# Gate products beside the latent attention: eight half passes in place of four whole ones

## The reference, cut to what matters

```python
h = rms_norm(x, g_mix)
z = h @ w_in
c_q, c_kv, k_rope, u2, q_nsa, kv_nsa, gate_nsa, gate_mix = jnp.split(z, SPLIT_IDX, axis=-1)
o_a = mla_mixer(c_q, c_kv, k_rope, ...)          # latent attention, 8 heads, causal, 512 x 512 scores
...
g_a, g_b, g_c = jnp.split(jax.nn.sigmoid(gate_mix.astype(jnp.float32)).astype(dt), N_MIXERS, axis=-1)
x = x + (g_a * o_a + g_b * o_b + g_c * o_c) @ w_out
```

## Time and profile before

| what | value |
|---|---|
| median of 3 runs | 3433.9 us (3432.43 to 3441.73) |
| the profiled execution, its own time | 3434.53 us |
| its span in the profile | 3432.7 us |
| PE busy, share of the span | 3374.2 us, 98% |
| PE weight loads busy | 2778.3 us, 81% |
| DVE, ACT, POOL busy | 59%, 42%, 46% |
| mean granted TensorE clock | 0.992 of full |
| chain that ended last, by engine | PE 83%, DVE 8%, ACT 5%, issue 2% |
| latent attention, layer 0 and layer 1 | from about 234 us and from about 1163 us on, some 50 us each |

### The profile page before, as it was taken

One profiled execution on the slowest core, in us unless ns is written; L12 is line 12 of the kernel. 1 busy time (PEld: TensorE's weight loads), 2 busy tenths in 40 slices (PEclk: granted clock), 3 DMA queues, 4 the chain that ended last, 5 costly groups with the idle time before them and its releaser, 6 DMA issues.

```text
span 3432.7 us, 44131 instructions
## 1 busy us (share of the span) xinstructions
PE 3374.2 (98%) x15776; PEld 2778.3 (81%) x15776; DVE 2018.2 (59%) x3204; ACT 1437.5 (42%) x2515; POOL 1587.8 (46%) x829
## 2 busy tenths in 40 slices
PE   9999999999999999999999999999999999999998
PEld 7877887888888778878888887888888877888887
DVE  6775666112367756751223676768964676768953
ACT  3256743332333567442323447333333447333332
POOL 3447454444434574644443641435544641435543
PEclk9999999999999999999999999999999999999999
DMA  4311123222332111322343221532344221432322
GB/s 173 110 56 44 38 93 111 98 98 94 107 114 99 50 44 50 115 94 96 109 145 124 69 87 56 179 128 98 134 138 146 68 87 50 173 134 104 134 94 103
DMA packets 96890, 346.65 MB, mean 101 GB/s; under 512 B 12640, under 2 KB 13408, under 8 KB 96096
## 3 DMA queue, kind: packets, MB, share of 16 engines
q1 hardware_dynamic: 96736, 344.62, 29.1%
HBM read 338.15 MB, written 6.29 MB: 100 GB/s over the span
## 4 chain that ended last, share of the span: by engine, by line
PE 83%; DVE 8%; ACT 5%; issue 2%; SPq 1%; POOL 0%; DMA 0%; ACTq 0%; DVEq 0%; POOLq 0%
PE ps L392 41%; PE ps L817 15%; PE ps L1425 4%; PE ps L550 4%; ACT arena L1298 3%; PE ps L403 3%; DVE split L1269 2%; PE ps L1705 2%; PE ps L1205 1%; PE ps L789 1%; PE ps L1915 1%; DVE ps L1261 1%; PE ps L805 1%; PE ps L1228 1%; PE ps L461 1%
## 5 line engine op out<-in xcount | busy, mean ns | idle before, releaser
L315 POOL TENSOR_TENSOR weights_lo<-arena,weights_hi 128x1024 fp32r<-128x1024 f32 x462 | 1176.8, 2548 | 1450.6 <-ACT weights_hi L285 1349.7
L285 ACT ACTIVATE weights_hi<-arena 128x1024 fp32r<-128x1024 f32 x490 | 516.8, 1055 | 614.4 <-PE ps L817 354.9
L392 PE MATMUL ps<-moving_hi,weights_hi 128*128 128x512 f32 x2144 | 536.5, 392 | 3.3 <-ACTq L278 1.8
L392 PE MATMUL ps<-moving_lo,weights_hi 128*128 128x512 f32 x2144 | 531.0, 390 | 0.0
L392 PE MATMUL ps<-moving_hi,weights_lo 128*128 128x512 f32 x2144 | 529.9, 389 | 0.0
L392 PEld LDWEIGHTS ps<-moving_hi,weights_hi 128*128 128x128 f32 x2144 | 399.7, 188 | 89.6 <-ACT weights_hi L285 4.0
L392 PEld LDWEIGHTS ps<-moving_hi,weights_lo 128*128 128x128 f32 x2144 | 402.2, 188 | 82.8
L392 PEld LDWEIGHTS ps<-moving_lo,weights_hi 128*128 128x128 f32 x2144 | 401.3, 188 | 83.9 <-issue 1.0
L336 DVE TENSOR_TENSOR moving_lo<-arena,moving_hi 128x512 fp32r<-128x512 f32 x196 | 202.7, 1084 | 223.3 <-ACT moving_hi L331 223.2
L534 POOL TENSOR_TENSOR weights_lo<-arena,weights_hi 128x512 fp32r<-128x512 f32 x80 | 105.1, 1326 | 270.8 <-ACT weights_hi L285 185.7
L2719 DVE SCALAR_TENSOR_TENSOR arena<-ps,arena 128x512 f32 x64 | 44.1, 691 | 294.2 <-PE ps L392 272.6
(11 more groups left out here) (396 smaller groups left out, 5426.9 us busy)
## 6 DMA issues: line engine op xcount, KB each, us to landing
arena<-wstream SPq DMA_DIRECT2D x532, 512.0 KB, 3.3
arena<-modw SPq DMA_DIRECT2D x64, 512.0 KB, 3.7
arena<-modw_first SPq DMA_DIRECT2D x32, 512.0 KB, 4.0
layer_input<-arena SPq DMA_DIRECT2D x2, 2048.0 KB, 10.4
arena<-layer_input SPq DMA_DIRECT2D x2, 2048.0 KB, 8.1
arena<-xT SPq DMA_DIRECT2D x4, 512.0 KB, 5.3
outT<-arena SPq DMA_DIRECT2D x8, 256.0 KB, 2.1
arena<-con SPq DMA_DIRECT2D x1, 1285.0 KB, 10.1
```

What stands on the lines that cost most here:

```text
L285: m.nc.scalar.activation(m.w_hi[:, (base + j) % 2, :], slab(m, base + at), ACT.Copy).then_inc(hi_ready, 1)
L315: m.nc.gpsimd.tensor_tensor(m.w_lo[:, n, :], slab(m, base + (j if at is None else at)), m.w_hi[:, n, :].bitcast(F32), ALU.subtract)\
L392: mm = m.nc.tensor.matmul(bank, unit_tile(w, k), a[:, k, :], start=(p == 0 and k == 0), stop=(p == 2 and k == KD - 1))
```

## The change

`product` takes a range of the eight tiles of `h`, so that a pass can be issued in two halves of four matmuls; the waits go to the first half and the signal to the last. The inner passes are placed half by half: half n stands at unit n * NU // (2 * inner). With 8 units and 4 inner passes that is one half beside each of the units 0 to 7. With 16 units and 16 inner passes both halves of a pass stand at one unit, as the whole pass did.

```diff
-    def product(self, pe, n):
+    def product(self, pe, n, part=range(KD)):
...
-            if p == 0:
+            if p == 0 and part[0] == 0:
                 pe.wait_ge(self.hi_ready, j + 1)
...
-            if p == 2:
+            if p == 2 and part[0] == 0:
                 pe.wait_ge(self.lo_ready, 2 * j + 2)
...
-            for k in range(KD):
+            for k in part:
...
-            if p == 2:
+            if p == 2 and part[-1] == KD - 1:
                 mm.then_inc(self.done, 1)
...
-        unit_of = [-1] + [n * NU // inner for n in range(inner)] + [NU]
+        halves = range(0, KD // 2), range(KD // 2, KD)
+        half_at = [n * NU // (2 * inner) for n in range(2 * inner)]
+        unit_of = [-1] + half_at[1::2] + [NU]
...
             def passes(u):
-                for n in range(inner + 2):
-                    if unit_of[n] == u:
-                        fill.product(pe, n)
+                if u in (-1, NU):
+                    fill.product(pe, 0 if u < 0 else inner + 1)
+                for n in range(2 * inner):
+                    if half_at[n] == u:
+                        fill.product(pe, 1 + n // 2, halves[n % 2])
```

## The result

The changed kernel took 3442.85 us (median of 12 runs, 3434.41 to 3450.45), the kernel before beside it 3436.14 us (12 runs, 3432.43 to 3441.73): a ratio of 1.002 with a 95% interval of 1.0012 to 1.0028, so 4 to 10 us slower, 6.7 us by the medians. Forecast was +1.9 us. The profiled execution took 3442.50 us with a span of 3440.7 us, 8.0 us over the span of before. The page shows nothing of it: busy shares and the chain's shares are those of before to the percent (PE 98%, chain PE 83%, DVE 8%, ACT 5%). Only the mean granted clock differs, 0.989 against 0.992.

What follows compares the result with a forecast made beforehand. The prediction took an ACT and DVE loop to bound the latent attention's middle and PE its end. 2 layers x (0 + 0.95) = +1.9 us on a median of 3433.9 gave 3435.8 us, range 3431.0 to 3440.0.

Steps and rivals of the forecast that it cites:

- The middle costs or gives nothing.: Latent attention, units 0 to 6: the ACT and DVE loop of 5.88 us a unit sets the pace; 0 us.
- Rival (a): Middle of the latent attention: PE sets the pace, even spread closes three waits a layer; -3.6 us, 3430.3 us, chance 0.07.
- The end: Units 6 and 7: four products moved between `product(6)` and `turn(7)` lengthen the path by 0.95 us a layer, bounds 0 to 1.11.
- The wait in front of `product(6)` grows from 1.19 to about 2.1 us.: Stage end: the four products leave the place before unit 6's transposes, where PE would wait anyway.
- Rival (c): Both latent attention stages: PE's clock falls below 0.86 of full, the change slower by over 0.3% (10.3 us); chance 0.04.
- A sign that I had in hand: Low stretch in the earlier trace, clock 0.65 of full: eight products of 1.81 us took 2.61, used to price Rival (c).
- The range: Whole kernel's median time: 3431.0 to 3440.0 us, leaving out Rival (c), most of Rival (a) and the tail of the scatter.

Runs made afterwards that it cites:

- kernel 1: Changed kernel with the last inner half moved back from unit 7 to unit 6; 3434.11 us against 3435.15 for the kernel before, ratio 0.9998.
- kernel 12: kernel 10 with whole passes beside every second unit again, without the even spread; 3430.36 us against 3435.38 for the kernel before, ratio 0.9985.
- kernel 4: Changed kernel with six idle matmuls of constants in PE's wait before `product(6)`; 3438.60 us against 3435.15 for the kernel before, ratio 1.0010.
- kernel 2: Changed kernel with whole passes at units 0, 2, 4 and only the last pass split over units 6 and 7; 3439.66 us against 3435.15 before, ratio 1.0019.
- kernel 5: Changed kernel with the four products at unit 7 not computed; 3439.22 us against 3435.01 for the kernel before, ratio 1.0018.
- kernel 9: Kernel before the change with the front stage's sixteen narrow matmuls issued in two pieces; 3435.97 us against 3436.09, ratio 1.0000.
- kernel 10: kernel 8 with the front stage's sixteen narrow matmuls issued in two pieces; 3428.99 us against 3436.09 for the kernel before, ratio 0.9978.
- kernel 8: Changed kernel, no half at unit 7, half the last pass issued in PE's wait before `product(6)`, likewise `product(14)` in 16-unit stages; 3433.49 us against 3435.01 before, ratio 1.0000.
- kernel 6: Changed kernel with two products at unit 7 in place of four; 3437.51 us against 3435.01 for the kernel before, ratio 1.0007.

## Why the prediction was wrong

- **"The middle costs or gives nothing."** Right. The loop kept its 5.83 and 5.93 us, the clock stayed at 1.00 there, and kernels 1 and 12 show from both sides that the spread has no price and no worth above the 3 us or so that the times can tell. The order I laid out holds in the trace: `product(1)` at 252.16 is 1.5 us before the exponentials at 253.66 (I had 1.7), the transposes start at +0.98 (I had 1.0), the scores at +2.07 (2.1). The first tile's copy to SBUF in unit 3 was covered by the wait for DVE as forecast. Rival (a) is out.
- **"The end", the moved work.** Right in size: 0.95 us of issue a layer. With the clock at full (kernel 4) the tails are 7.24 and 7.28 against 6.48, so 0.8: the four products take 284.71 - 283.72 = 0.99 us, and `product(6)`, which starts late there and has its second half ready, takes 1.40 instead of 1.59.
- **"The wait in front of `product(6)` grows from 1.19 to about 2.1 us."** Right (2.10 and 2.09), and this is the step that failed: I wrote the wait down as harmless, "where PE would wait anyway". It has a price of its own. Behind it the clock is granted below full in both layers, at 0.72 over six microseconds, and the tail grows by a further 9.01 - 6.48 - 0.95 = 1.58 and 8.68 - 6.49 - 0.95 = 1.24 us. The term that I gave 0.95 with an upper bound of 1.11 measured 2.53 and 2.19, in all 4.7 us where I had 1.9. Of the ten stage ends with a wait of 2.1 us or more in five profiles, nine had a low clock behind it; of the eighteen with a shorter or a filled wait in nine profiles, none. Kernel 2 (the wait without the spread), 4 (the spread without the wait) and 5 (the wait without the work) show it.
- **Rival (c)** had the right mechanism at the wrong place and with the wrong price. It asked how far the clock must fall before PE's 5.48 us pass the loop's 5.88, which is a question of the middle, where PE has slack. At the end the chain is PE's, as I had written myself, and each microsecond of missing clock there counts at once. What (c) named, more than 0.3%, did not come. I weighed the clock against many small pauses, found 1.00 with pauses of 0.9 and 1.2 us in the stage, and gave it 0.04. But the change also makes one pause longer than any that row covers, and I did not ask what that one would do. The rule of the Trainium skill (TensorE: Matmul & The Clock Gate, "A second HAM failure mode: psum-queue depth-cycling") that frequent short idles make the clock swing is not what happened: the short pauses of the even spread left it at 1.00, one of 2.1 us did not. By that rule kernel 1 should have been slow and kernel 2 not; it was the reverse.
- **A sign that I had in hand.** The low stretch of the earlier trace rows was in the profile of before, and I took its price from it without reading what PE did ahead of it. It had been idle for 1.56 us and had then issued one wide matmul and eight matmuls with one column:

```profile
594.84 0.50 PE L403 MATMUL ps<-moving_lo,weights_hi 128*128 128x512 f32 x1 [1.56 <-DVE moving_lo L2703]
595.18 0.95 PE L2644 MATMUL ps<-arena 128*128 128x1 f32 x8
595.99 2.97 PE L403 MATMUL ps<-moving_lo,weights_hi 128*128 128x512 f32 x8
```

The same pause of 1.56 us stands in both layers of all fourteen profiles, and a low clock came behind it in 17 of the 28 cases. So pauses under 2.1 us are not free everywhere, and the profile of before already had a pause with a low clock behind it.

- **The remaining 2 us** of the 6.7 by the medians lie inside the interval (4 to 10), so they may be scatter. The change's profile has low stretches at 104, 948 and 1036 us that the profile of before has not, and lacks one that the profile of before has (1524 us). The one at 104 us comes before any changed instruction, so the change cannot have caused it. In ten profiles with the sixteen narrow matmuls in one piece the clock was low behind them in 7 of 20 layers, in four profiles with two pieces in 0 of 8; if the pieces made no difference, such a split would still come by chance about once in 25 times. Kernel 9 shows no gain from this edit by itself.
- **The range** ended at 3440.0, 4 us over my number, and was drawn round 3433.9, the median of three runs; twelve runs of the same kernel gave 3436.14. The measured 3442.85 would have been outside by less, but still outside, with that base. The prediction also took 0.3%, 10.3 us, for the least that can be told from no change; with twelve runs a side, 6.7 us were told.

## What to carry to other kernels

When work is moved out of a place where the busiest engine waits, the wait it leaves behind must be priced, not only the work where it lands: here a 1.2 us pause in front of the stage's end was free in every profile, and a 2.1 us pause cost 1.2 to 1.6 us more each time the clock fell. Where a profile shows a low clock, read what the engine did ahead of it, not only what the stretch cost. A bubble in front of the instruction that the end of a stage hangs on is the place to put independent work into; four products there shortened each stage end by 0.7 to 0.9 us in the trace, though the time showed it only together with the split sums (kernels 10 and 12). Spreading work evenly beside a loop that another pair of engines paces gave nothing here.

## What the runs showed of the hardware

- The scatter of this kernel's runs goes with the clock. Over the 110 runs of the kernel before that stand beside the experiments, time and mean granted clock have a correlation of -0.90: runs at 0.989 have a median of 3439.7 us, at 0.991 of 3435.4, at 0.993 of 3431.2, about 2.3 us for each 0.001. In kernel 8, with eleven runs and a clock 0.001 lower, a gain of 5 us in the trace was not told from nothing.
- Whether the clock falls at a given place differs from one execution to the next and from layer to layer of one execution, with the same instructions and the same wait (kernel 5: 2.12 us in both layers, a fall in one). One profile does not show that a place is safe.
- Ahead of a low clock PE did one of three things in the places read here: it was idle for 2.1 us or more right behind ten transposes (9 of 10); it was idle for 1.56 us and then issued one wide matmul and eight matmuls with one column (17 of 28); or it issued sixteen matmuls with one column in one piece, during which the page counts it as busy (7 of 20). The other low stretches, most of them from 1866 us on and in every kernel, were not read, so this is no full list. It also means that no single length of pause decides: the profile of kernel 6 has no fall behind 1.65 us in front of `product(6)` and one behind 1.56 us in both layers.
- The Trainium skill says of transposes (TensorE: Matmul & The Clock Gate, "Part 4: PE-mode transpose") that they do not count as activity for the clock as other matmuls do. That would fit the first case, but no run here moved the transposes away from the wait, so it stays open whether they matter.
- Still open: why kernel 10 is 7.1 us faster than the kernel before, where its ends give 5.0 as those of kernel 12 do, and why kernel 8 showed so little of it. Their intervals (0.9969 to 0.9988, 0.9976 to 0.9994, 0.9989 to 1.0010) overlap or nearly touch; the narrow matmuls in two pieces are the only edit between 8 and 10, but the same edit did nothing by itself in kernel 9.
